# Second block's mixers: the fourth pair's recurrent gate products stand between the two first output-gate units instead of ahead of both

## What is computed

```python
h = rms_norm_2(x, mix_norm[l])
proj = h @ w_in[l] + b_in[l]
q, k, v, f_logit, xr, gr, g_attn, g_rnn = jnp.split(proj, SPLIT_POINTS, axis=-1)
...
xr = causal_depthwise_conv(xr, conv_w[l], conv_b[l])
yr = rg_lru(xr, lru_w_a[l], lru_b_a[l], lru_w_x[l], lru_b_x[l], lru_lambda[l]) * jax.nn.gelu(gr)
y_rnn = yr @ w_o_rnn[l]
merged = jax.nn.sigmoid(g_attn) * y_attn + jax.nn.sigmoid(g_rnn) * y_rnn
```

```python
r = jax.nn.sigmoid(block_diag_linear(x, w_a, b_a))
i = jax.nn.sigmoid(block_diag_linear(x, w_x, b_x))
log_a = -LRU_C * r * jax.nn.softplus(-lam)
a = jnp.exp(log_a)
u = jnp.sqrt(-jnp.expm1(2.0 * log_a)) * (i * x)
# h = a * h_before + u over the positions
```

## Time and profile before

| | |
|---|---|
| median of 3 runs | 3329.25 us (3327.9 to 3329.63) |
| profiled execution | 3328.07 us |
| its span, first to last instruction | 3326.3 us |
| PE busy | 3307.3 us, 99% |
| DVE, POOL, ACT busy | 65%, 64%, 44% |

### The profile page before, as it was taken

The page is one execution under the profiler, slowest core; times in us unless marked ns, Lnnn a source line. Parts: engine busy times, 40 slices in busy tenths (PEclk is TensorE's granted clock), DMA queues, the critical chain, the costliest instruction groups (busy, mean ns, idle before and its releaser), DMA issues.

```text
span 3326.3 us, 52762 instructions
## 1 busy us (share of the span) xinstructions
PE 3307.3 (99%) x17742; PEld 2799.6 (84%) x17742; DVE 2169.0 (65%) x3377; ACT 1466.9 (44%) x2025; POOL 2128.9 (64%) x2188
## 2 busy tenths in 40 slices
PE   9999999999999999999999999999999999999999
PEld 5888777888889997788888899889987888888998
DVE  8887685544478878714435877788878334248886
ACT  4365664222243335735634333433347545533333
POOL 6444445555568886653356888698876544468886
PEclk9999999999999999999999999999999999999999
DMA  6221553322232223332223323232223222223232
GB/s 223 88 70 64 166 183 108 104 95 96 98 111 94 107 82 102 102 127 70 70 83 110 108 101 113 76 114 101 101 89 109 95 102 70 83 92 111 102 109 100
DMA packets 94485, 343.36 MB, mean 103 GB/s; under 512 B 10609, under 2 KB 11249, under 8 KB 93954
## 3 DMA queue, kind: packets, MB, share of 16 engines
q1 hardware_dynamic: 86978, 312.11, 27.3%
q10 hardware_dynamic: 7360, 29.29, 2.7%
HBM read 335.03 MB, written 2.13 MB: 101 GB/s over the span
## 4 chain that ended last, share of the span: by engine, by line
PE 52%; POOL 23%; issue 19%; ACT 2%; DVE 2%; DVEq 1%; ACTq 0%; POOLq 0%; DMA 0%; SPq 0%
POOL w_lo L588 22%; PE ps L634 15%; PE ps L636 15%; PE ps L635 15%; POOL t_lo L588 1%; PE ps L1217 1%; PE ps L1199 1%; PE ps L801 1%; PE ps L802 1%; PE ps L803 1%; PE ps L1208 0%; ACT w_hi L1305 0%; DVE arena L2771 0%; DVE arena L2172 0%; POOL xres L567 0%
## 5 line engine op out<-in xcount | busy, mean ns | idle before, releaser
L588 POOL TENSOR_TENSOR w_lo<-raw,w_hi 128x256 fp32r<-128x256 f32 (+1 forms) x1680 | 1468.4, 906 | 1051.5 <-ACT w_hi L1305 1049.3
L634 PE MATMUL ps<-a_hi,w_lo 128*128 128x512 f32 (+1 forms) x2720 | 1019.4, 375 | 1.6 <-ACT arena L1315 0.8
L636 PE MATMUL ps<-a_hi,w_hi 128*128 128x512 f32 (+1 forms) x2720 | 1005.5, 370 | 0.0
L635 PE MATMUL ps<-a_lo,w_hi 128*128 128x512 f32 (+1 forms) x2720 | 1005.1, 370 | 0.0
L588 POOL TENSOR_TENSOR w_lo<-arena,w_hi 128x512 fp32r<-128x512 f32 x384 | 586.2, 1552 | 124.3 <-ACT w_hi L1785 121.2
L634 PEld LDWEIGHTS ps<-a_hi,w_lo 128*128 128x128 f32 x2720 | 512.5, 188 | 102.8 <-issue 18.3
L1305 ACT ACTIVATE w_hi<-raw 128x1024 fp32r<-128x1024 f32 x374 | 392.6, 1053 | 442.0 <-PE ps L636 423.4
L636 PEld LDWEIGHTS ps<-a_hi,w_hi 128*128 128x128 f32 x2720 | 512.6, 188 | 88.0
L635 PEld LDWEIGHTS ps<-a_lo,w_hi 128*128 128x128 f32 x2720 | 513.0, 189 | 81.2 <-issue 0.5
L634 PE MATMUL ps<-b_hi,w_lo 128*128 128x512 f32 x1088 | 425.8, 391 | 4.7 <-DVE b_lo L2190 4.0
L635 PE MATMUL ps<-b_lo,w_hi 128*128 128x512 f32 x1088 | 424.2, 390 | 0.0
(11 more groups left out here) (332 smaller groups left out, 4707.1 us busy)
## 6 DMA issues: line engine op xcount, KB each, us to landing
raw<-in_stream SPq DMA_DIRECT2D x471, 512.0 KB, 3.3
arena<-in_stream SPq DMA_DIRECT2D x96, 512.0 KB, 3.4
arena<-in_mod_w ACTq DMA_DIRECT2D x32, 512.0 KB, 4.1
arena<-in_mod_w SPq DMA_DIRECT2D x16, 512.0 KB, 11.6
arena<-arena ACTq DMA_DIRECT2D x16, 256.0 KB, 3.7
arena<-cum_rows ACTq DMA_DIRECT2D x2, 2048.0 KB, 7.9
xres<-in_x_t SPq DMA_DIRECT2D x4, 512.0 KB, 5.4
arena<-in_first SPq DMA_DIRECT2D x8, 256.0 KB, 11.8
```

Of the source, the lines that this page charges most:

```text
L588: last = pool.tensor_tensor(to[:, at], of[:, at], hi[:, at].bitcast(F32), ALU.subtract)
L634: pe.matmul(out, lo, x_hi, start=start, stop=False)
L635: pe.matmul(out, hi, x_lo, start=False, stop=False)
L636: return pe.matmul(out, hi, x_hi, start=False, stop=stop)
```

## The change

In the list of PE's work for each of the two layers, the two calls that `gates()` made are written out, and `lru_gates(3)` moves between them. The bodies of the functions stay as they are.

```diff
                 units_of(bank_a)
                 lru_gates(2)
                 units_of(bank_a)
+                project(bank_a())
                 lru_gates(3)
-                gates()
+                project(bank_a())
 
                 queries_keys_values(0, lambda n: None)
```

## The result

The changed kernel takes 3334.52 us in the median of 20 executions (3333.21 to 3335.70), the kernel before 3328.40 us in the median of 20 (3327.38 to 3329.63): +6.1 us, a ratio of 1.0018 with a 95% interval of 1.0011 to 1.0025. The span of the profiled execution is 3331.9 us, 5.6 us longer than before.

What follows compares the result with a forecast made beforehand. PE, busy 99% of the span, was taken to bound the kernel. Nothing won ahead of the place and 2.50 us lost behind it per layer gave +5.0 us on 3329.25, so 3334.2 us, range 3331.0 to 3336.8.

Steps and rivals of the forecast that it cites:

- What bounds the kernel: Whole kernel: PE is busy 99% of the span, so any time it stands still is added to the end.
- Part 1: Ahead of the moved products: an eviction wait takes the place of the DMA wait at the same price, 0.0 us won.
- Part 2: Behind the moved products: ACT's first tanh 2.50 us late, first query unit 2.20 us late behind a 2.0 us hole.
- Part 3: Later in the stage: the loss is kept, growing from 2.20 to 2.50 us at the inverse-root wait (L767).
- The sum: Both layers together: 2 x 2.50 = +5.0 us, bounds +4.4 and +5.6, forecast 3334.2 us.
- A: Behind the new hole PE's clock falls to half: 3337.2 us if in both layers, 3335.7 if in one; chance 0.06.
- B: POOL's low weights for the second query unit come late: +0.6 us a layer, 3335.4 us; chance 0.06.
- C: Not slower: first query unit not bound to ACT's gate activations, or later slack absorbs the delay; with D, chance 0.08.
- D: At ACT's first tanh: something else also held it at 1379.63, so the claimed delay fails; with C, chance 0.08.
- The chances: Whole kernel: within 0.2% of before 0.85, slower by more 0.14, faster by more 0.01; forecast range itself 0.80.

Runs made afterwards that it cites:

- null: Kernel before with the two calls of gates() written out, same instructions in the same order: 3328.49 us, +0.05 us against the kernel before.
- first_layer: Changed kernel with the move made in the first layer only: 3331.17 us, +2.7 us against the kernel before.
- inside_g0: Changed kernel with the gate products behind 12 of the first output-gate unit's 24 matmuls: 3328.39 us, -0.05 us against the kernel before.
- act_matched: Changed kernel with ACT evicting the first output-gate unit before the fourth pair's gate activations: 3336.06 us, +7.8 us against the kernel before.
- behind_g1: Changed kernel with the gate products one unit further back, behind both output-gate units: 3346.77 us, +18.3 us against the kernel before.
- after_again: The changed kernel itself, unaltered, timed again beside the kernel before: 3333.88 us, +5.3 us.
- gelu_first: Changed kernel with ACT's first gelu eviction of the fourth pair ahead of a rounding: 3331.87 us, +3.6 us against the kernel before.

## Why the prediction was right

**What bounds the kernel.** Right: PE loses what it idles, and nothing behind the place gave it back. The changed kernel's trace is 3.1 us late behind the first place and 3.0 ahead of the second, 5.6 behind that and 5.6 at the end. The null kernel and first_layer tie the loss to the place.

**Part 1.** Right: G0 waits 0.82 us for gr0's eviction where L1167 had waited 0.84 for the DMA. That this is neutral by itself is shown by inside_g0.

**Part 2.** Right, with two small errors. I let ACT start 0.04 us behind the last gate product; it is 0.08 (1380.73 + 1.95 = 1382.68, ACT at 1382.76). So the tanh is 2.55 to 2.56 us late instead of 2.50. Q0 idles 1.90 us as forecast and is 2.24 us late instead of 2.20.

**Part 3.** Right: the loss grows from 2.24 at Q0 to 2.53 us at L767, whose wait is 0.67 us instead of the 0.9 I gave, since PE itself is 2.43 us late by the first L767 (1398.33 before, 1401.34 after, less the 0.58), not 2.20. The prediction left out that PE's matmuls are slower just behind a hole: the second one starts 0.33 us after the first (1390.24, 1390.57), where 0.23 us is the step in the dense row (1387.42 to 1387.65 before), and some more follow at 0.23 to 0.24.

In the second layer, which the prediction took over from the first, L767 shows no wait at all, before or after. It still starts 0.05 us behind the end of the inverse root in both kernels. Before:

```profile
2601.73 0.50 PE L767 MATMUL ps<-sq_split,neg_tri 128*128 128x512 f32 x1
...
2601.05 0.63 ACT L1360 ACTIVATE arena<-arena 128x512 f32<-128x512 f32 x1
```

After:

```profile
2607.29 0.49 PE L767 MATMUL ps<-sq_split,neg_tri 128*128 128x512 f32 x1
...
2606.60 0.63 ACT L1361 ACTIVATE arena<-arena 128x512 f32<-128x512 f32 x1
```

So both ways to L767, PE's own over Q0's wait and the chain over ACT and DVE, are late by about the same 2.5 us. act_matched shows that the chain alone is enough to carry the loss; which of the two carries it in the changed kernel's second layer stays open.

**The sum.** +5.0 us forecast, 5.1 us in the trace, +6.1 and +5.3 us in two measurements. The predicted 3334.2 us lie 0.3 us from the median, but that it is so near is luck, because two errors cancel: the 3329.25 us from which I started are 0.85 us above the median of 20 executions, and the difference is 0.3 to 1.1 us larger than I said.

**The rivals.** A was judged wrongly. I gave it 0.06 and took the fall as settled by the hole's length; it happens in some executions and not in others, at a hole of 1.90 us, and it is the likely reason of the spread upwards and of what the medians have above the 5.1. "Likely", since it is seen in one of two traces of this kernel and in that of gelu_first, and for the other executions only the mean clock speaks. B did not happen: PE shows no wait for POOL at Q1. C and D are refuted by behind_g1 and by the 2.56 us.

**The chances.** The measured change, +0.18%, is inside the 0.2% that I had called unchanged, its interval reaches over it, and its sign is that of the forecast.

## What to carry to other kernels

Before moving a product to fill a wait of the bounding engine, look at who consumes the product, and at how long the product has been ready when that engine arrives: here it was ready 3.2 us before ACT came, the move made it 5.7 us later, and the difference of 2.5 was lost whole. A wait on the bounding engine is worth removing only if the next waits downstream do not grow by the same; here the waits of Q0 and for the root took back 0.5 of 0.8 us. And a queue in hand-written order ties things together that have nothing to do with each other: the eviction that freed PE's bank stood behind a tanh that waited for PE.

## What the runs showed of the hardware

PE's clock can fall behind a hole that the trace gives as 1.90 us, at the same place of the same program in one execution and not in another: of the seven such holes in the traces of the changed kernel, after_again, gelu_first and first_layer, the granted clock fell behind two, for 3.4 us and at a cost of 1.3 us. Behind the holes of 2.68 and 1.99 us in act_matched it did not fall in the profiled execution (granted clock 1.00 from 1402 to 1408 us), behind 3.95 us it did in every trace, and behind 7.56 us in both layers. How long it stays down varies too: behind the same 3.95 us it was 3.4 us in eight traces and 6.8 us in four, which cost 0.9 to 1.2 us more. The Trainium skill, page "TensorE: Matmul & The Clock Gate", part on the HAM clock gate, says that activity releases the throttle, and these traces agree: the granted clock is 0.5 behind each hole of 3.95 us and comes back to 1.00 while PE multiplies. They add that a hole's length alone does not decide.

Where the instruction behind a table load on ACT had one wait in this program, as at 1378.91, the load stood ahead of the wait, which hid it. In act_matched the eviction had two (for PE's products and for DVE), and one of them was put on the table load itself (1382.06, 1.97 us idle, then 1.28 us of load): there the load came behind the wait and onto the chain.
